# Stage ends in four quarters, the order of the latent attention, and a forget-gate projection on four column tiles

## The reference, cut to what matters

```
h = h + short_conv(rms_norm(h))          # w_in 1024x3072, w_out 1024x1024
h = h + swiglu(rms_norm(h))              # w13 1024x5632, w2 2816x1024
h = h + mla(rms_norm(h))                 # latents 384 and 256+64, 8 heads, causal
h = h + swiglu(rms_norm(h))
x = rms_norm(h)
proj = rms_norm_2(x) @ w_in              # 1024 x 2336; 32 of the columns are zf and zb
log_a = log_sigmoid(z @ up + bias) / 16  # z: 256 x 16 for each direction, up: 16 x 256
h = x + [gla(...), gqa(...)] @ w_out
h = h + hier_moe(rms_norm_2(h))          # 64 experts of three 1024x512 matrices
out = rms_norm_2(h)
```

## Time and profile before

| | us |
|---|---|
| median of 3 runs | 1586.71 |
| the profiled execution | 1586.83 |
| its span | 1585.0 |
| PE busy | 1297.7 |
| DVE busy | 547.3 |
| ACT busy | 445.3 |
| POOL busy | 54.2 |

### The profile page before, as it was taken

One profiled execution on the slowest core, in us unless ns is written; L12 is line 12 of the kernel. 1 busy time (PEld: TensorE's weight loads), 2 busy tenths in 40 slices (PEclk: granted clock), 3 DMA queues, 4 the chain that ended last, 5 costly groups with the idle time before them and its releaser, 6 DMA issues.

```text
span 1585.0 us, 29674 instructions
## 1 busy us (share of the span) xinstructions
PE 1297.7 (82%) x12725; PEld 971.7 (61%) x12725; DVE 547.3 (35%) x931; ACT 445.3 (28%) x764; POOL 54.2 (3%) x70
## 2 busy tenths in 40 slices
PE   9999999999999999999677667666666666676665
PEld 9989999878999987865344334334333334334332
DVE  6776555776655679541001000010010010010001
ACT  6444444665444456531011011011011011011101
POOL 1000000001000034000000000000000000000000
PEclk9999999999999999999889888899989899889888
DMA  9645554434655537599999999999999999999997
GB/s 374 237 160 192 183 208 139 174 139 146 212 192 201 170 118 292 198 425 429 429 432 432 431 432 430 432 432 431 432 430 431 432 431 432 430 431 432 432 431 307
DMA packets 46180, 519.91 MB, mean 328 GB/s; under 512 B 5393, under 2 KB 5553, under 8 KB 8754
## 3 DMA queue, kind: packets, MB, share of 16 engines
q1 hardware_dynamic: 45218, 517.87, 80.0%
q0 software_dynamic: 480, 0.96, 0.2%
q10 hardware_dynamic: 432, 0.38, 0.1%
HBM read 518.14 MB, written 1.05 MB: 328 GB/s over the span
## 4 chain that ended last, share of the span: by engine, by line
DMA 47%; PE 44%; DVE 4%; ACT 2%; issue 1%; SPq 0%; POOL 0%; POOLq 0%; ACTq 0%; DVEq 0%
DMA work<-in_moe_units 23%; DMA ring<-in_moe_units 23%; PE ps L338 10%; PE ps L340 10%; PE ps L339 10%; PE ps L2252 4%; PE ps L2261 3%; DMA ring<-in_conv_units 1%; DVE w_split L279 1%; ACT w_split L275 1%; PE ps L2295 1%; PE ps L2275 1%; PE ps L479 0%; DVE xT_lo L559 0%; PE ps L986 0%
## 5 line engine op out<-in xcount | busy, mean ns | idle before, releaser
L2252 PE MATMUL ps<-ring,work 128*32 128x256 f32 x2976 | 203.1, 419 | 92.9 <-DMA ring<-in_moe_units 92.8
L338 PE MATMUL ps<-xT_hi,w_split 128*128 128x256 f32 x960 | 266.7, 278 | 1.8 <-DVE xT_lo L559 1.4
L2479 DVE TENSOR_TENSOR work<-ps,work 128x128 f32<-128x128 f32 x64 | 18.7, 292 | 717.9 <-ACT work L2392 717.9
L339 PE MATMUL ps<-xT_lo,w_split 128*128 128x256 f32 x960 | 265.5, 277 | 0.0
L340 PE MATMUL ps<-xT_hi,w_split 128*128 128x256 f32 x960 | 265.4, 276 | 0.0
L279 DVE TENSOR_TENSOR w_split<-ring,w_split 128x2048 fp32r<-128x2048 f32 (+3 forms) x100 | 225.7, 2259 | 86.5 <-ACT w_split L275 85.2
L275 ACT ACTIVATE w_split<-ring 128x2048 fp32r<-128x2048 f32 (+3 forms) x104 | 194.2, 1870 | 133.3 <-PE ps L340 128.7
L2252 PEld LDWEIGHTS ps<-ring,work 128*32 128x32 f32 x2976 | 95.4, 118 | 190.0 <-DMA ring<-in_moe_units 119.1
L338 PEld LDWEIGHTS ps<-xT_hi,w_split 128*128 128x128 f32 x960 | 180.3, 188 | 4.4 <-issue 3.3
L339 PEld LDWEIGHTS ps<-xT_lo,w_split 128*128 128x128 f32 x960 | 180.4, 188 | 0.9
L340 PEld LDWEIGHTS ps<-xT_hi,w_split 128*128 128x128 f32 x960 | 180.3, 188 | 0.0
(11 more groups left out here) (360 smaller groups left out, 1567.1 us busy)
## 6 DMA issues: line engine op xcount, KB each, us to landing
ring<-in_moe_units SPq DMA_DIRECT2D x124, 2048.0 KB, 26.8
ring<-in_ffn_units SPq DMA_DIRECT2D x66, 1024.0 KB, 4.8
x_slots<-in_moe_units SPq DMA_DIRECT2D x32, 2048.0 KB, 25.7
work<-in_moe_units SPq DMA_DIRECT2D x32, 2048.0 KB, 26.8
ring<-in_conv_units SPq DMA_DIRECT2D x14, 1024.0 KB, 12.5
ring<-in_win_units SPq DMA_DIRECT2D x9, 1024.0 KB, 4.8
ring<-in_wo_units SPq DMA_DIRECT2D x4, 1024.0 KB, 5.6
kept_slot<-in_moe_units SPq DMA_DIRECT2D x2, 2048.0 KB, 14.8
```

The costliest lines, as they stand in the source:

```text
L338: pe.matmul(out_ap, stat_hi, mov_hi, start=first, stop=False, skip_group_check=True)
L339: pe.matmul(out_ap, stat_hi, mov_lo, start=False, stop=False, skip_group_check=True)
L2252: last = pe.matmul(ps[CAP * j:CAP * j + CAP, b, 0:BLK], xstat[:, 4 * half + k, CAP * lane:CAP * lane + CAP], w[k][:, j // 2, BLK * (j % 2) ...
L2479: dve.tensor_tensor(astat[par], bank(b, 256).rearrange("p (c s j m) -> p c s j m", c=2, s=2, j=2)[:, :, 1, :, :], wk(SI, 128).rearrange("p ...
```

## The change

At the four ends named (not at `mix`) the last unit's quarters come in the order (0,0), (1,0), (0,1), (1,1). After the third, PE transposes the left four chunks of both token tiles (`turn_left`); the right four follow in the next stage (`turn_right`), tile 0 ahead of its first products and tile 1 after the first six of them. DVE adds in four pieces of 512 (`sum_half`), and the lo parts of pairs 0 and 1 stand ahead of and behind the fourth piece. ACT makes pairs 0 and 1, squares tile 0, makes pairs 2 and 3, squares tile 1. The first unit of the next stage takes its chunks pair by pair for both of its outputs. `aT` moves to the other half of `xS`, so that the new pairs don't meet it.

In the attention, the transposes of the query latents stand inside `latents(1)`; DVE's mean for the norm moves ahead of the second operand's lo parts; the rotated queries go to banks 4 and 5, and their wait goes from ahead of `scores(0)` to its second half; ACT splits unit u+9 ahead of reading the rotated queries and DVE ahead of `maxima(0)`; `maxima(t+1)` stands behind the normalisation of head t for odd t; `keep_busy` goes.

In the last block, the gate unit holds 32 columns instead of 160 per chunk. It is multiplied from `raw` in fp32, without hi and lo of the weights: 2 halves x 2 operand parts x 4 column tiles = 16 fp32 matmuls of 32 stationary columns and 256 moving ones, each tile summing its two chunks. Tile sums are joined by an `up` matrix whose rows are repeated for the tiles (128 rows, half of them zero for each direction). DVE scales all 128 partitions with one instruction, ahead of `ahead_lo(u + 2)`. The split of unit U_WIN+2 moves into `end1`, and the factor broadcast moves behind unit 2. SP waits for the gate unit's products before it loads unit U_WIN+9 over its place.

```diff
+    HALVES = [(0, 0), (1, 0), (0, 1), (1, 1)]
+    def by_token_last(pe, u, x, chunks, prev, tag):
+        unit_ready(pe, u)
+        hi, lo = weights(u, 2, D)
+        for g, (tt, part) in enumerate(HALVES):
+            if g == 3:
+                turn_left(pe, prev, tag)
+            cs = slice(512 * part, 512 * part + 512)
+            for q, ch in enumerate(chunks):
+                last = passes(...)
+            if g < 3:
+                last.then_inc(s("all_acc"), 1)
+        last.then_inc(s("used"), 1)
+    def turn_left(pe, prev, tag):
+        pe.wait_ge(*mark(f"{prev}_h", 2))
+        for k in range(KD // 2):
+            for tt in range(TT):
+                last = pe.transpose(bank(k // 2, P, (k % 2) * T + tt * P), h[:, tt, k * P:k * P + P], ident)
+            if k % 2:
+                last.then_inc(s("all_T"), 1)
+    def by_channel_first(pe, u, out_bank, x, prev, ready):
+        unit_ready(pe, u)
+        turn_right(pe, prev, 0)
+        hi, lo = weights(u, KD, 256)
+        for pair in range(KD // 2):
+            pe.wait_ge(*mark(ready, pair + 1))
+            for f in range(2):
+                for k in (2 * pair, 2 * pair + 1):
+                    last = passes(...)
+                if pair == f == 0:
+                    turn_right(pe, prev, 1)
+        last.then_inc(s("used"), 1)
+    def next_stage_dve(dve, units_done, prev, split, tag, gain, dst):
+        sum_half(dve, prev, 0, units_done)
+        lo_half(dve, split, 0)
+        sum_half(dve, prev, 1, units_done)
+        sum_half(dve, prev, 2, units_done)
+        operand_dve(dve, tag, NORM_BANKS, gain, dst, pairs=[0])
+        sum_half(dve, prev, 3, units_done)
+        operand_dve(dve, tag, NORM_BANKS, gain, dst, pairs=[1])
+        lo_half(dve, split, 1).then_inc(s("raw_read"), 1)
+        operand_dve(dve, tag, NORM_BANKS, gain, dst, pairs=[2, 3])
...
     def scores(pair):
...
+            if pair == 0:
+                pe.wait_ge(s("qpt"), 2)
             for tt in range(TT):
                 n = P * (tt + 1)
                 q0 = QPT + T * pair + P * tt
...
-        pe.wait_ge(s("qpt"), 2)
         scores(0)
...
-        keep_busy(pe, 4, 5)
         keys(u + 9, 4)
...
     def head(t):
-            if t + 1 < HEADS:
+            if t % 2 == 0 and t + 1 < HEADS:
                 maxima(t + 1)
...
+            if t % 2 and t + 1 < HEADS:
+                maxima(t + 1)
...
         halves(1, 4, 0)
+        halves(2, 4, 1)
         rstd_rows_pe(pe, "n1", 0)
-        halves(2, 4, 1)
         unit_ready(pe, u + 3)
-        hi, lo = weights(u + 3, KD, 160)
-        for z in range(2):
-            for k in range(KD):
-                last = passes(pe, bank(6, T, T * z), hi[:, k, 16 * z:16 * z + P], lo[:, k, 16 * z:16 * z + P],
-                              xT_hi[:, k, :], xT_lo[:, k, :], k == 0, k == KD - 1)
+        w = raw[:, (u + 3) % RAW, 0:KD * ZW].rearrange("p (k c) -> p k c", c=ZW)
+        for half in range(2):
+            for x in xT:
+                for j in range(QUAD):
+                    k = QUAD * half + j
+                    last = pe.matmul(ps[ZW * j:ZW * j + ZW, Z_BANK, 0:T], w[:, k, :], x[:, k, :].bitcast(F32), start=half == 0 and x is xT_hi,
+                                     stop=half == 1 and x is xT_lo, skip_group_check=True)
...
     def win_dve(dve):
         u = U_WIN
-        ahead_lo(dve, u - 1)
+        ahead_lo(dve, u)
         rstd_rows_out(dve, "n1", 0)
-        for q in range(2):
-            ahead_lo(dve, u + q)
+        ahead_lo(dve, u + 1)
         qk_squares_dve(dve)
-        ahead_lo(dve, u + 2)
...
+        dve.tensor_tensor(wk(ZT, T), bank(Z_BANK, T), rb[:, :], ALU.mult).then_inc(s("zt"), 1)
+        ahead_lo(dve, u + 2)
         ahead_lo(dve, u + 3)
...
-            pool.dma_start(up[:, 0, :], a["gla_up_fwd_2"][0]).then_inc(s("params"), 16)
-            pool.dma_start(up[:, 1, :], a["gla_up_bwd_2"][0]).then_inc(s("params"), 16)
+            pool.dma_start(up[:, :, :], a["up_rows"]).then_inc(s("params"), 16)
```

More of the change, by code:

```diff
@@ L43 @@
 QUAD = P // CAP
+ZW = 32
 BIG_NEG = -3.0e38
@@ L541, in rb2, with operand_act @@
         return rb[:, None, :].broadcast_to([P, n, T])
-    def operand_act(act, tag, psum_tag, banks, gain, dst, first=0, at=0, also=None):
+    def operand_act(act, tag, psum_tag, banks, gain, dst, first=0, at=0, also=None, pairs=None):
         for b, (pb, n) in enumerate(banks):
+            if pairs is not None and b not in pairs:
+                continue
             act.wait_ge(*mark(psum_tag, at + b + 1))
@@ L552, in operand_act, with operand_dve @@
             last.then_inc(s("all_hi"), 1)
-    def operand_dve(dve, tag, banks, gain, dst, first=0):
+    def operand_dve(dve, tag, banks, gain, dst, first=0, pairs=None):
         for b, (pb, n) in enumerate(banks):
+            if pairs is not None and b not in pairs:
+                continue
             dve.wait_ge(*mark(f"{tag}_hi", b + 1))
@@ L1306, in program @@
     LAST = (CH - 1, 0)
+    KV_BANK, Z_BANK = 6, 7
     def win_pe(pe):
         u = U_WIN
-        other_rows(pe, "ffn2", "n1")
-        by_token(pe, u, [[bank(7, 256, 256 * tt)] for tt in range(TT)], xT, range(KD), KD, 256, 256, True, True, ready="n1x_lo")\
-            .then_inc(s("used"), 1)
+        unit_ready(pe, u)
+        turn_right(pe, "ffn2", 0)
+        hi, lo = weights(u, KD, 256)
+        for pair in range(KD // 2):
+            pe.wait_ge(*mark("n1x_lo", pair + 1))
+            for tt in range(TT):
+                for k in (2 * pair, 2 * pair + 1):
+                    last = passes(pe, bank(KV_BANK, 256, 256 * tt), xT_hi[:, k, tt * P:(tt + 1) * P], xT_lo[:, k, tt * P:(tt + 1) * P],
+                                  hi[:, k, :], lo[:, k, :], k == 0 and tt == 0, k == KD - 1)
+                if pair == tt == 0:
+                    turn_right(pe, "ffn2", 1)
+        last.then_inc(s("used"), 1)
         def halves(unit, b, q):
@@ L1435, in win_act @@
         u = U_WIN
-        for q in range(3):
-            ahead_hi(act, u - 1 + q)
+        for q in range(2):
+            ahead_hi(act, u + q)
         act.wait_ge(s("used"), u + 3)
@@ L2733, in packed_weights @@
     w = v["w_in_2"][0]
-    out["win_gate_units"] = columns(w, [1536], 160)
+    out["win_gate_units"] = columns(w, [1536], ZW)
+    up = np.zeros((P // ZW, 2, ZW // 2, 2, 256), np.float32)
+    for d, name in enumerate(("gla_up_fwd_2", "gla_up_bwd_2")):
+        up[:, d, :, d, :] = v[name][0]
+    out["up_rows"] = up.reshape(P, 2, 256)
     halves_of = lambda at: rows(w[:, at:at + 512], every(D, 512), 512)
```

161 lines of the change are left out of this document (90 added, 71 removed).

## The result

The changed kernel takes 1578.94 us (median of 5 runs, 1577.97 to 1579.03), the kernel before 1586.71 beside it (5 runs, 1586.51 to 1586.95): ratio 0.9949, interval 0.9936 to 0.9963. That is 7.8 us less, where 10.7 were predicted (1576.0), and inside the range of 1573.2 to 1580.2. The profiled execution took 1578.94, its span 1577.1.

A forecast was written before the change was run, and what follows sets the result against it. PE was taken to bound the kernel up to about 658 us, a fixed transfer stream after. 1.4 + 3.2 + 1.8 + 2.0 + 2.7 - 0.2 = 10.9 off 1586.83 gave 1575.9, stated as 1576.0; range 1573.2 to 1580.2.

The forecast's parts named there:

- DVE follows late: Rival: DVE's lo parts at stage ends or splits in the attention bind; only 6 us saved, 1580.5; chance 0.12.
- the upper gain: Rival: the attention gives all of its 5.8 and unit 4's split is not waited for; 1572.5; chance 0.08.
- The regimes and the fixed stream: PE full up to about 660 us, then transfers saturated with fixed bytes; PE's savings before 658 us move the end equally.
- Stage ends: Turns from one stage to the next: 1.4 saved at conv to ffn1, 1.8 attention to ffn2, 2.0 ffn2 to last block.
- A cost of 0.2 for `up`'s load: Near 24 us the wider `up` load goes out while transfers are saturated: 0.2 us lost, bounds 0 and 0.5.
- Attention with its entrance: Entrance gives 1.5; with the reordered transposes, splits and maxima and no filler, 3.2 us saved in sum, bounds 1 and 5.
- The last block: Smaller gate unit saves PE 3.8; waiting about 1.1 for unit 4's lo part leaves 2.7 us net.
- POOL holds the last block: Rival: PE waits for POOL's turned queries, so only 1.7 of the last block's 4.7 remain; 1579; chance 0.12.
- The clock falls: Rival: without the filler the attention's clock could fall, half rate over 328 to 369 us costing 41; 1617; chance 0.03.

The follow-up runs named there:

- e5: Changed kernel with the attention's inner order put back as before, stage ends, entrance and last block kept as changed: 1581.05 us, ratio 0.9965.
- e2: Changed kernel with the last block's gate unit, `up` matrix, factor broadcast and order of splits put back as before: 1579.54 us, ratio 0.9957.
- e4: Changed kernel without POOL's rotation of the second attention's queries and keys: 2517.06 us, not comparable, since a second round of experts runs.
- e8: Changed kernel with POOL's 16 multiplications started beside DVE's squares instead of after them: 1578.70 us, ratio 0.9949.
- e6: Changed kernel with the factor broadcast between unit 2's token tiles and ACT reading half its copies of keys and values earlier: 1576.87 us, ratio 0.9938.
- e3: Changed kernel with DVE's lo part of unit 8 ahead of the 16 scans instead of behind them: 1579.64 us, ratio 0.9958.

## Why the prediction came out as it did

Up to the product with `up` each term came in within 0.25 but the attention's (0.7 short), and the time lies in the range. But what put it 2.9 above the forecast was no case of mine: the range held it by its width, taken from the cases of POOL and DVE, and not because I saw this loss. Slips in the rivals' sums change nothing: DVE's case, 4 + 0.5 + 2, is 6.5 and gives 1580.2, not 1580.5, and the upper gain, 2.6 and 1.1 more, gives 1572.3, not 1572.5.

**The regimes and the fixed stream**: right. Load and end moved together (8.19 and 7.9).

**Stage ends**: right, as far as the traces before and after show it; no run undid them by themselves. Conv, from the ready sums to the clearing: 95.48 to 107.01 before, 94.93 to 104.91 after, 1.55 for the 1.4 forecast. Attention to ffn2: PE's lead on the kernel before grew from 4.63 (369.07 and 364.44) to 6.65 (380.34 and 373.69), by 2.02 (forecast 1.8); ffn2 to the last block from 6.65 (554.55 and 547.90) to 8.82 (565.81 and 556.99), by 2.17 (2.0). A cost of 0.2 for `up`'s load can't be seen: it would lie in the 0.55 by which the two traces differ at 95 us.

**Attention with its entrance**: 2.5 for 3.2. The waits are mostly those foreseen. The lead at the last output units is 4.6, 2.1 of it from conv's end and from the traces' start. The sum "entrance 1.5, order 1.7" was the wrong picture, as e5 shows, with nearly the right total; 0.50 of the shortfall of 0.7 is the new wait at 336.34.

**The last block**: this is the step that failed, and only in part. Its rows came in: 1.94 for the gate unit (1.8), a wait of 0.85 (1.1), the product with `up` at 576.88 (577.5). The lead grew by 2.73 up to there (2.7). Counted from the 6.65 ahead of the last end, the product came 4.90 earlier (4.7) and the squares 1.69 (1.65). What I wrote of the queue behind the waiting copy, "DVE's split of unit 4 and the squares of the queries, which start 1.65 earlier instead of 4.7", I followed to POOL alone. The same squares start DVE's own chain to the lo part of unit 8, where PE already waited 0.67 before, so DVE and not PE set that start. The sum has no term for it: PE ran 3.2 ahead of DVE, DVE made up 3.49 of idling and lost 2.06 beside POOL, and PE's lead fell from 11.55 to 9.76. That is 1.8 for a term that I had at nothing, and 1.56 more where the clock fell behind the wait. At full clock the whole gate part is worth 1.3 to 1.5 in the traces instead of 2.7 (e2), with the reserve on its medians said there.

**The rivals.** DVE follows late: its place was wrong (hardly in the ends or the attention) and its mechanism right; it took 1.8 us. POOL holds the last block: POOL was ready at 600.1 and PE came at 605.2, so it held nothing, but it acted by slowing DVE (e4), which I hadn't thought of. The clock falls: in one profile it did, for 1.56 us behind the longer wait and not in the attention, where 0.85 of idling without the filler left it full. No case of mine had the three joined.

## What to carry to other kernels

When a part makes PE faster, write down for each later wait which engine sets it and when that engine's own chain starts; a lead of PE beyond that start is lost. An edit at the head of a chain can be worth nothing as long as the order behind it stays old (the entrance alone 0.07, both 2.5), so undo such edits one by one before giving each a price. Work of GpSimd and VectorE that begins to overlap can cost both; the one move tried here (e8) only changed who paid, while an earlier start of VectorE's chain (e6) gave 1.6.

## What the runs showed of the hardware

DVE and POOL slow each other by the kind of DVE's instruction. Beside POOL's additions of 0.88 to 0.93 a scan of 64 columns takes 0.91, about one POOL instruction, and 0.26 alone; two fp32 splits take 5.18 for 4.50; a square of two tiles 2.12 for 1.56. The sums along groups (one input) take 1.55 in e8 beside POOL and 1.54 in e4 without it, and the product that reads one input from PSUM 1.21 to 1.22 in both. A product with two inputs in SBUF takes 1.65 for 1.23. POOL in turn took 19.1 for its sixteen multiplications in e3 and 18.2 in e8, for 17.0, and 4.44 for 2.39 (e3). The rows of eight hide how it goes: in the changed kernel a multiplication of 64 columns takes 0.32 or 0.33 where it isn't held up, but this one, beside the first of the two splits (575.49 to 578.34), lasts to the end of it:

```profile
576.16 2.36 POOL L1619 TENSOR_TENSOR work<-work 128x64 f32<-128x64 f32 x1
```

Who pays differs. In the kernel before, two splits beside POOL's multiplications kept their 2.28 and 2.27 while two of POOL's took 2.45 and 3.25 (for some 0.33 and 0.75); in the changed kernel the first split took 2.85 as well. So an overlap has no fixed price. The "GPSIMD Engine Reference" of the Trainium skill, Specifications, says that the two engines share SBUF interfaces and contend where a DVE instruction has two SBUF inputs or uses both ports. The traces agree for two SBUF inputs. A scaling with one input in SBUF (L1645) is slowed too, 0.81 for 0.68 in e4; whether that is the other case no run here shows. The prices are these rows'.

TensorE's clock behind a wait inside full work, one execution each: behind 1.41, 1.97, 2.24, 2.60 and 2.63 us of idling it stayed at 1.00, behind 2.54 and 3.42 it fell to 0.53 to 0.62 of full for some 4 us. 2.54 and 2.63 are the same kernel's, so the length of the wait alone doesn't decide.
